# Second block: the gate-up product takes x without the norm's reciprocal root, which is multiplied onto each tile as it leaves PSUM

## The reference, cut to what matters

```python
def _rmsnorm(x, w):
    y = x * lax.rsqrt(jnp.mean(x * x, axis=-1, keepdims=True) + NORM_EPS)
    return y * w

def _conv_glu_ffn(h, ffn_up, ffn_conv, ffn_conv_bias, ffn_down):
    u = _causal_dwconv(h @ ffn_up, ffn_conv) + ffn_conv_bias    # 3 taps along the tokens
    gate, val = jnp.split(u, 2, axis=-1)                         # 2816 channels each
    return (jax.nn.gelu(gate, approximate=True) * val) @ ffn_down

# second_block, one layer
h = _hybrid_mixer_2(_rmsnorm(x, pre_mix_norm[l]), ...)
x = x + _rmsnorm(h, post_mix_norm[l])
h = _conv_glu_ffn(_rmsnorm(x, pre_ffn_norm[l]), ...)
x = x + _rmsnorm(h, post_ffn_norm[l])
```

## Time and profile before

| | |
|---|---|
| median of three runs | 1983.71 us |
| the profiled execution: time, span | 1979.94 us, 1978.1 us |
| busy share of the span: PE, DVE, ACT, POOL | 95%, 61%, 50%, 36% |
| mean granted TensorE clock | 0.975 |
| chain that ended last, by engine | PE 68%, DVE 10%, ACT 8%, DMA 6%, issue 5%, POOL 2% |
| bytes read from HBM | 309.61 MB |

### The profile page before, as it was taken

One profiled execution on the slowest core, in us unless ns is written; L12 is line 12 of the kernel. 1 busy time (PEld: TensorE's weight loads), 2 busy tenths in 40 slices (PEclk: granted clock), 3 DMA queues, 4 the chain that ended last, 5 costly groups with the idle time before them and its releaser, 6 DMA issues.

```text
span 1978.1 us, 40944 instructions
## 1 busy us (share of the span) xinstructions
PE 1880.3 (95%) x15728; PEld 1842.6 (93%) x15728; DVE 1214.3 (61%) x1480; ACT 993.4 (50%) x1301; POOL 722.0 (36%) x607
## 2 busy tenths in 40 slices
PE   6999999999999999999999998997999889979997
PEld 6999999999999999999999997987999889969997
DVE  5655586666556545676665566556774755647754
ACT  4434565454454345555544456455654464556542
POOL 4760211257317621303376102513661105215631
PEclk9999999999999999999999989998999889999999
DMA  6646444455465556344464633222555323215543
GB/s 228 201 167 212 171 150 150 154 194 205 157 206 192 184 165 210 129 153 168 171 210 156 200 136 107 86 86 86 199 185 165 135 104 107 87 50 180 196 153 125
DMA packets 48938, 312.33 MB, mean 158 GB/s; under 512 B 5680, under 2 KB 6832, under 8 KB 19888
## 3 DMA queue, kind: packets, MB, share of 16 engines
q1 hardware_dynamic: 48096, 307.84, 45.6%
q10 hardware_dynamic: 720, 2.84, 0.4%
HBM read 309.61 MB, written 1.05 MB: 157 GB/s over the span
## 4 chain that ended last, share of the span: by engine, by line
PE 68%; DVE 10%; ACT 8%; DMA 6%; issue 5%; POOL 2%; ACTq 0%; DVEq 0%; SPq 0%; POOLq 0%
PE ps L558 18%; PE ps L559 18%; PE ps L560 18%; DMA raw<-in_down_dram 4%; ACT w_hi_w L1215 4%; DVE w_lo_w L1695 4%; PE ps L915 3%; PE ps L563 3%; PE ps L565 3%; PE ps L564 3%; DMA raw<-in_in_dram 1%; DVE v L2244 1%; DVE conv L2023 1%; PE ps L726 1%; PE ps L766 1%
## 5 line engine op out<-in xcount | busy, mean ns | idle before, releaser
L1695 DVE TENSOR_TENSOR w_lo_w<-raw,w_hi_w 128x2048 fp32r<-128x2048 f32 (+1 forms) x288 | 616.3, 2140 | 303.0 <-ACT w_hi_w L1215 302.3
L558 PE MATMUL ps<-xn,w_hi_w 128*128 128x256 f32 x2688 | 762.6, 284 | 39.9 <-DVE xn L1709 26.4
L559 PE MATMUL ps<-xn,w_hi_w 128*128 128x256 f32 x2688 | 753.8, 280 | 0.0
L560 PE MATMUL ps<-xn,w_lo_w 128*128 128x256 f32 x2688 | 753.6, 280 | 0.0
L1215 ACT ACTIVATE w_hi_w<-raw 128x2048 fp32r<-128x2048 f32 (+1 forms) x288 | 497.8, 1730 | 141.0 <-DMA raw<-in_down_dram 89.9
L558 PEld LDWEIGHTS ps<-xn,w_hi_w 128*128 128x128 f32 x2688 | 515.9, 192 | 47.8 <-DVE xn L1709 24.1
L559 PEld LDWEIGHTS ps<-xn,w_hi_w 128*128 128x128 f32 x2688 | 514.6, 191 | 0.6 <-issue 0.5
L560 PEld LDWEIGHTS ps<-xn,w_lo_w 128*128 128x128 f32 x2688 | 514.2, 191 | 0.0
L558 PE MATMUL ps<-h,w_hi_w 128*128 128x256 f32 x1056 | 294.2, 279 | 3.0 <-DVE w_lo_w L1695 3.0
L560 PE MATMUL ps<-h,w_lo_w 128*128 128x256 f32 x1056 | 293.8, 278 | 0.0
L559 PE MATMUL ps<-h,w_hi_w 128*128 128x256 f32 x1056 | 293.8, 278 | 0.0
(11 more groups left out here) (336 smaller groups left out, 2822.1 us busy)
## 6 DMA issues: line engine op xcount, KB each, us to landing
raw<-in_gu_dram SPq DMA_DIRECT2D x132, 1024.0 KB, 4.9
raw<-in_in_dram SPq DMA_DIRECT2D x68, 1024.0 KB, 4.9
raw<-in_down_dram SPq DMA_DIRECT2D x96, 704.0 KB, 4.1
raw<-in_out_dram SPq DMA_DIRECT2D x16, 1024.0 KB, 4.8
raw<-in_pb_dram SPq DMA_DIRECT2D x4, 1024.0 KB, 4.9
raw<-in_pa_dram SPq DMA_DIRECT2D x4, 1024.0 KB, 4.9
tables_all<-in_tables_dram ACTq DMA_DIRECT2D x1, 1648.0 KB, 6.8
rows<-in_rows_dram SPq DMA_DIRECT2D x2, 768.0 KB, 5.5
```

What stands on the lines that cost most here:

```text
L558: pe.matmul(out, w, xh, start=first, stop=False)
L559: pe.matmul(out, w, xl, start=False, stop=False)
L560: return pe.matmul(out, wl, xh, start=False, stop=last)
L1695: dve.tensor_tensor(in_ring(w_lo_ring, at, k)[:, 0:elems], raw[:, k % RAW_RING, 0:elems], in_ring(w_hi_ring, at, k)[:, 0:elems], ALU.subtr ...
```

## The change

ACT now makes the high part of `x * gain` as soon as a chunk of x is there (`split_x`, together with the square), and DVE the low part (`scale_low`) inside `post(1)`; the two engines' second pass with `v` is gone, and POOL's part of it. POOL sums the eight squares (`post_square`), and PE multiplies that sum by one matmul between the two tiles of slot 1 instead of eight matmuls ahead of slot 0. The split of slot 2 (`open_rounds`) stands ahead of the root. In each round DVE first multiplies both tiles by `rstd` from PSUM into `conv_in`, and the second of these signals `drained`; the taps of ACT and DVE then read `conv_in`.

The core of the diff (the counts of semaphores and removed helpers are left out):

```diff
             mean_square(at, 0)
-            mean_square_direct(at, 1)
             first_wide(at, st2["gu"], 0)
+            def mean_of_x():
+                pe.wait_ge(post_sum.sem, post_sum.upto(at, KC - 1))
+                pe.matmul(ps[:, AUX, 0:T], ones_d[:], sq8[:, 0], start=True, stop=True).then_inc(mean_sq.sem, 1)
-            wide(at, st2["gu"], 1, 0, xn, KC)
+            wide(at, st2["gu"], 1, 0, xn, KC, None, mean_of_x)
...
             src = conv_in[:, j % 2, f]
+            if f == 0:
+                before = 6 if st.name == "gu" else 0
+                act.wait_ge(conv_src.sem, conv_src.upto(at, before + j + 1 + 4 * g))
+            else:
+                act.wait_ge(drained.sem, drained.upto(at, st.free0 + j + 1 + 4 * g))
             if st.name == "gu":
-                tile_done(act, at, st, j, f, g)
-                src = ps[:, 2 * (j % 2) + f, 0:T]
...
+                act.sem_inc(held.sem, 1)
...
             for c in range(KC):
                 x_ready(act, at, 0, c)
+                split_x(c, gains2[:, 4 * layer + 2, c:c + 1])
                 act.activation(sq8[:, c], x[:, c], ACT.Square).then_inc(squared.sem, 1)
+            open_rounds(at, st2["gu"], split)
             root(at, 2)
-            for c in range(KC):
-                act.wait_ge(v_ok.sem, v_ok.upto(at, c + 1))
-                copy(xn[:, c, 0], v[:, c]).then_inc(xn_hi.sem, 1)
...
-                whole = st.name == "gu"
-                if not whole:
-                    for f in range(2):
-                        tile_done(dve, at, st, j, f, g)
-                        dve.tensor_tensor(conv_in[:, j % 2, f], ps[:, 2 * (j % 2) + f, 0:T], rstd[:, 0:T], ALU.mult)\
-                           .then_inc((conv_src, drained)[f].sem, 1)
+                for f in range(2):
+                    tile_done(dve, at, st, j, f, g)
+                    dve.tensor_tensor(conv_in[:, j % 2, f], ps[:, 2 * (j % 2) + f, 0:T], rstd[:, 0:T], ALU.mult)\
+                       .then_inc((conv_src, drained)[f].sem, 1)
+                dve.wait_ge(drained.sem, drained.upto(at, st.free0 + j + 1 + 4 * g))
...
-                        src = ps[:, 2 * (j % 2) + f, 0:T - s] if whole else conv_in[:, j % 2, f, 0:T - s]
-                        ins = dve.scalar_tensor_tensor(c, src, w(f, last_tap - s), c, ALU.mult, ALU.add)
+                        dve.scalar_tensor_tensor(c, conv_in[:, j % 2, f, 0:T - s], w(f, last_tap - s), c,
+                                                 ALU.mult, ALU.add).then_inc(conv_ok.sem, 1)
...
                 def scale_next(c):
-                    if k == 3 and layer < DEPTH - 1:
+                    n = k // 2
+                    if k == 1 or layer < DEPTH - 1:
...
             split(at, so.slot0 + 3 + LEAD, 0, SLOT)
+            open_rounds(at, st2["gu"], split)
             inverse(at, 2)
-            for c in range(KC):
-                dve.scalar_tensor_tensor(v[:, c], x[:, c], gains2[:, 4 * layer + 2, c:c + 1], rstd[:, 0:T],
-                                         ALU.mult, ALU.mult).then_inc(v_ok.sem, 1)
-                if c >= 2 and c % 2 == 0:
-                    low_even(at, 0, c - 2)
-            low_even(at, 0, KC - 2)
...
-            add_odd(at, 0)
-            for c in range(1, KC, 2):
-                low(at, 0, c)
+            def post_square(c):
...
+                pool.tensor_tensor(sq8[:, 0], sq8[:, 0], sq8[:, c], ALU.add).then_inc(post_sum.sem, 1)
+            add_odd(at, 0, {3: (1,), 5: (2, 3), 7: (4, 5, 6, 7)}, post_square)
```

More of the change, by code:

```diff
@@ L362, in program @@
     col_ok = sig("col_ok", 0, 1)
-    v_ok = sig("v_ok", 0, KC)
+    post_sum = sig("post_sum", 0, KC - 1)
     post_v = sig("post_v", 0, 2 * KC)
@@ L421, in program @@
     tap = sig("tap", 0, 12 + 2 * FC)
-    conv_ok = sig("conv_ok", 0, 36 + 3 * FC)
-    conv_src = sig("conv_src", 0, 6)
+    conv_ok = sig("conv_ok", 0, 36 + 4 * FC)
+    conv_src = sig("conv_src", 0, 6 + FC)
     z_ok = sig("z_ok", 0, 1)
@@ L1668, in gelu @@
             def gelu(j, g):
-                act.wait_ge(conv_ok.sem, conv_ok.upto(at, 36 + 3 * j + 3 + 12 * g))
+                act.wait_ge(conv_ok.sem, conv_ok.upto(at, 36 + 4 * j + 3 + 16 * g))
                 act.activation(silu_gate[:, j % 2], conv[:, j % 2, 0], ACT.Gelu_apprx_tanh).then_inc(gate_ok.sem, 1)
             act.activation(warm[:, 3:4], eps[:, 0:1], ACT.Gelu_apprx_tanh)
-            open_rounds(at, st2["gu"], split)
             rounds(act, at, st2["gu"], SLOT_DOWN, FC, split, gate_taps, gelu)
@@ L2003, in taps @@
             def taps(st, j, g, w, slots0, conv0, last_tap):
-                whole = st.name == "gu"
-                if not whole:
-                    for f in range(2):
-                        tile_done(dve, at, st, j, f, g)
-                        dve.tensor_tensor(conv_in[:, j % 2, f], ps[:, 2 * (j % 2) + f, 0:T], rstd[:, 0:T], ALU.mult)\
-                           .then_inc((conv_src, drained)[f].sem, 1)
-                    dve.wait_ge(drained.sem, drained.upto(at, st.free0 + j + 1))
-                per = 2 * last_tap - (1 if whole else 0)
+                for f in range(2):
[3 more added lines that the diff above has]
+                dve.wait_ge(drained.sem, drained.upto(at, st.free0 + j + 1 + 4 * g))
+                if st.name == "gu":
+                    dve.sem_inc(held.sem, 1)
+                per = 2 * last_tap
                 for s in range(1, last_tap + 1):
@@ L2238, in scale_next @@
                 def scale_next(c):
-                    if k == 3 and layer < DEPTH - 1:
-                        x_ready(dve, at, 1, c)
-                        scale_low(at, 1, c, gains2[:, 4 * (layer + 1), c:c + 1], xn_lo_odd if c % 2 else xn_lo_even)
+                    n = k // 2
+                    if k == 1 or layer < DEPTH - 1:
+                        x_ready(dve, at, n, c)
+                        scale_low(at, n, c, gains2[:, 4 * layer + k + 1, c:c + 1], xn_lo_odd if c % 2 else xn_lo_even)
                 for c in range(KC):
@@ L2291, in add_square @@
             pool.tensor_tensor(ssum[:], ssum[:], sqb[:, c % 2], ALU.add).then_inc(summed.sem, 1)
-        def low(at, n, c):
-            pool.wait_ge(xn_hi.sem, xn_hi.upto(at, KC * n + c + 1))
-            pool.tensor_tensor(xn[:, c, 1], v[:, c], xn[:, c, 0], ALU.subtract).then_inc(xn_lo_odd.sem, 1)
         def add_squares(at, k):
@@ L2448, in _ @@
             add_squares(at, 0)
-            add_odd(at, 0)
-            for c in range(1, KC, 2):
-                low(at, 0, c)
+            def post_square(c):
+                pool.wait_ge(squared.sem, squared.upto(at, KC + c + 1))
+                if c > 1:
+                    pool.wait_ge(post_sum.sem, post_sum.upto(at, c - 1))
+                pool.tensor_tensor(sq8[:, 0], sq8[:, 0], sq8[:, c], ALU.add).then_inc(post_sum.sem, 1)
+            add_odd(at, 0, {3: (1,), 5: (2, 3), 7: (4, 5, 6, 7)}, post_square)
             split_h(at, st2["gu"], 0)
```

13 lines of the change are left out of this document (1 added, 12 removed).

## The result

The changed kernel takes 2000.96 us (median of 9 runs, 1992.7 to 2010.72), the kernel before 1983.71 us (9 runs, 1977.83 to 1990.25). The ratio is 1.0081, 95% interval [1.0056, 1.0105]: slower by about 16 us, outside the range forecast. The profiled execution has a span of 1999.6 us, 21.5 us more than before, at a granted clock of 0.976 (0.975 before).

The account below looks back on a forecast made before the run. PE's idle wait at each gate-up entry was taken as the bound. A layer: -3.5 at the entry, +1.3 in the rounds, +0.5 at the end, makes -1.7 us; two layers -3.4, so 1980.3 us from 1983.7; range 1974 to 1990.

Parts of the forecast that it names:

- the ring: Each gate-up round: DVE split, drain, ACT tap, ACT split, DVE split; 5.40 us, or 5.49 with the `held` count.
- A round, worked from 'qkv': Part reckoning a gate-up round from stage "qkv": 5.50 us against PE's 5.43, 18 times a layer, +1.3 us.
- The entry: Gate-up's start: first matmul 5.7 us after R, the mixer norm's reciprocal, instead of 14.2; slot 1 at R + 17.2.
- What slot 3 wins: Start of gate-up's slot 3: 3.5 us earlier a layer, or 4.4 us if POOL's two adds cost nothing.
- Drain to tap: Step of the ring from DVE's drain to ACT's tap: 0.45 us, plus 0.09 for the `held` count.
- Two taps to ACT's split: Step of the ring from the first of ACT's two taps to its split: 0.81 us, read from "qkv".
- DVE's own way and the collision: DVE's line through a gate-up round: 4.93 us, 5.49 with POOL's subtraction (0.46) and cast (0.1) beside its taps.
- The rival with two collisions: Gate-up rounds: POOL and DVE collide twice, 5.85 us a round, 9.2 us lost in all, 1993 us; chance 13%.
- The end: End of gate-up, before PE resumes in "down": one added drain loses 0.5 us a layer, bounds 0 and 1.
- The clock: Rival: PE falls to half clock in gate-up's slot 1, costing 1.7 us a layer; 1983.7 us, no change; chance 8%.
- The bounds: Gate-up round between 5.43 us (PE's own) and 6.08 us (all three POOL instructions land on DVE's way).
- The sign I had named: Stated test in the profile after: the forecast is wrong if a gate-up round is over 5.6 us.

Follow-up runs that it names:

- e4: Changed kernel with ACT's 22 gate-up rounds written out instead of looped: 1995.45 us, rounds 5.67 to 5.68 us.
- e9: Changed kernel with ACT's gate-up taps made without the convolution's bias: 1980.38 us, rounds 5.60 us in the loop and 5.49 behind it.
- e2: Changed kernel without the `held` counts in the taps on ACT and DVE: 2000.4 us, round 5.81 us.
- e10: Changed kernel with e2 and e4 together (no `held` counts, ACT's rounds written out): 1993.25 us, round 5.66 us.
- e1: Changed kernel with POOL's subtraction for the low part of h replaced by a cast: 1989.06 us, round 5.88 us.
- e3: Changed kernel with e1 and e2 together (POOL's cast, no `held` counts): 1998.17 us, round 5.81 us.
- e12: e11 with POOL's subtraction replaced by a cast, as in e1: 1990.17 us, round 5.47 us.
- e5: Changed kernel's entry with the rounds of the kernel before (taps read PSUM, root left out): 1982.43 us, ratio 0.9982 to the kernel before.
- e11: e10 with ACT's taps made without their bias, as in e9: 1988.09 us, round 5.47 us.
- e8: Changed kernel, ACT splitting one slot further ahead, DVE splitting between drains and taps, and slot 1 during the mixer's last tiles: 1981.27 us, ratio 0.9986.

## Why the prediction was wrong

The mechanisms were named rightly, and two terms of the ring that sets the round were too small. Both lie in "A round, worked from 'qkv'", and the third miss, at the end of the stage, follows from it in the main.

- **The entry, right within 0.6 us.** First matmul R + 5.7 forecast, 5.72 measured; slot 1 R + 17.2 and 17.23, idle 1.8 and 1.77. The root came 0.3 us later than reckoned (1376.76, R + 20.70), and the drain of slot 0 at R + 23.28 instead of R + 22.7. The 0.9 us for POOL's squares is there, but only half of it ahead of the split of slot 1: four xn instructions took 3.58 us instead of 3.09, so the split began at R + 14.35, not 14.8, and then took 2.82 us (the one behind it 2.28). That slot 1 came out exact is luck in this respect.
- **What slot 3 wins, 3.5 forecast, 2.2 measured.** 0.6 us is the later drain, and 0.4 the ring's two steps below, which stand in that sum too. The remaining 0.36 is a misreading of the kernel before: the sum has slot 2 start when ACT saw slot 1 done, at 1377.7, but PE went on at 1377.32 without a wait.
- **Drain to tap, 0.54 forecast, 0.73 measured.** It was read from "qkv", whose six rounds are written out. 16 of the 22 rounds here stand in a loop, and there drain to tap is 0.20 us longer (e4): 0.09 of it is the bias's (e9) and about 0.05 the `held` count's, which costs 0.07 in the loop (e2) and 0.02 outside it (e10). The forecast's 0.09 for the count, read in "down", was near the first. But without loop and count the step is 0.51, where "qkv" has 0.45.
- **Two taps to ACT's split, 0.81 forecast, 1.00 measured.** The tap in "qkv" has a scale, the tap here a scale and a bias. Two take 1.09 us instead of 0.91, and e9 gets the 0.19 back. The row of the right instruction stood in the earlier trace rows: 0.57 us for one, against 0.91 for two in the earlier trace rows. I didn't set them beside each other. The Trainium skill (page "ScalarE: Activation LUTs", section "What ACT_TABLE_LOAD costs") has the same: each operand that is a pointer to one value per partition adds about 93 ns to an activation. The two taps here agree, with 0.09 us more for each of them. 0.20 + 0.19 is the whole difference between 5.49 and 5.88; that it comes out so exactly is chance in part, as the count was taken too high outside the loop and the 0.45 too low.
- **DVE's own way and the collision.** Forecast 1.58 us for the four taps and 0.56 for POOL, 2.14 in all; from start to start they take 2.16. Two errors cancel: in round 0, where POOL is idle, their row is 1.78 us long instead of some 1.66, and POOL adds 0.45 to it (2.23). As forecast, one tap of the four is lengthened, to 1.05 us from 0.47. The step from ACT's first tap to DVE's was 0.77 instead of 0.61 as well. None of it decides, since ACT's way got longer (e1, e3, e12). The rule of the Trainium skill on it (page "SBUF — State Buffer", section "Who interferes with whom") agrees: taps with both operands in SBUF take 0.45 us more beside POOL's subtraction, while taps that read the tile from PSUM take 0.40 us each beside it (three in 1.27 us, e5) and as much where POOL is idle (four in 1.65). Beside POOL's cast, which reads SBUF too, the four take 1.84 us (e1), hardly more than alone. The rival with two collisions didn't occur: POOL's `hv` (1389.34) still starts 0.43 us behind DVE's split (1388.91).
- **The end, 0.5 forecast, 3.1 measured** (a wait of 4.28 instead of 1.21). I added one drain to a chain that began when PE's last tile ended. But DVE and ACT are now late themselves: the last tile ends at about 1497.1, its drain starts at 1498.57, and all four taps follow the drain. Some 1.0 us of it goes where POOL's subtraction is a cast (e1; e3 against e2), so that part is the collision's. What PE has lost in the rounds isn't lost beside the end, but on top of it. Where DVE and ACT have caught up with PE, the forecast's 0.5 is right: in layer 0 of e11 PE resumes 5.4 us after the end of its last tile, against 4.9 before and 8.0 in the changed kernel.
- **The clock** didn't fall in slot 1 of this profile (granted 1.00), though it fell behind the wait at the end, where the sum has no term for it. But the rival was real: of the 22 layers with this entry and its 1.8 us wait in all profiles, five have half clock in slot 1 (e1 and e3 in layer 0, e11 in layer 1, e9 in both), and there slot 2 starts at R + 25.7 instead of R + 24.1, 1.6 us later, where the rival reckoned 1.7. e1 (columns as in the windows above):

```profile
1366.70:1370.20 3.50, 3.50 (x20) 3.50 (x19) 1.64 (x1) 0.00 (x0) 0.00 (x0) 0.51 0.82 279
```

- **The bounds.** The upper end of 6.08 us for a round held, but all of it was POOL's, and the range was cut at a round of 5.7 us. The sign I had named ("wrong if a round is over 5.6 us") is what the profile shows, and the sum follows it: -2.2 at slot 3, +7.5 by the last tile (15 x 0.45 + 3 x 0.24), +3.1 at the end, 8.4 us a layer and 16.8 for both. The medians differ by 17.3. Part of that agreement is chance, since the half clock behind the end (1.6 us a layer) and PE's pace aren't in the sum.

The slip of method: the margin was 0.03 us (5.40 against 5.43, before the count), the ring has four steps, and 18 rounds twice multiply an error by 36. Each of its steps had to be read from an instruction of the same form, operands and loop.

## What to carry to other kernels

When a change spends an engine's head start, reckon the ring of dependences that is then exposed, step by step from start to start, and take each step from an instruction with the same operands (scale, bias, source) and the same kind of code (looped or written out). A gain at the entry of a stage is paid once; a loss in its round is paid every round and once more at the end. And when two engines must each wait for the other's split in one round, move one of the splits a slot ahead before anything is added to the round.

## What the runs showed of the hardware

TensorE has two paces at one granted clock. Windows in one SwiGLU stage of the first block, which is the same code in both kernels, first before, then after (same columns as above):

```profile
1100.00:1110.00 10.00, 10.00 (x91) 10.00 (x90) 5.60 (x5) 4.86 (x5) 0.74 (x1) 1.00 0.48 152
```

```profile
1100.00:1110.00 10.00, 10.00 (x87) 10.00 (x87) 5.37 (x7) 5.56 (x7) 0.74 (x1) 1.00 0.61 200
```

The granted clock is 1.00 in both, but 91 matmuls fall into 10 us in one and 87 in the other; their starts lie 0.113 and 0.118 us apart (1104.78 to 1106.48 in 15 steps; 1104.77 to 1106.42 in 14). One stage keeps one pace for most of its length, and which one it gets changes from stage to stage and run to run with no edit: this stage took 183.9 us between its norms' reciprocals before and 189.7 after. That is about the 5.5 us by which R was late in this comparison. In e5 the same stage took 189.7 us and R of layer 0 is 1370.61 instead of 1350.57, though its edit lies behind R. It is why the length of a round tells more than a whole time. The cause stays open. The Trainium skill (page "TensorE: Matmul & The Clock Gate", section "Wait — 56ns, not 53.3ns?") gives matmuls at the full clock their columns at 2.4 GHz and about 2.5 ns. An estimate from these figures is 109 ns for 256 columns; both paces measured here are slower than that. Where the ring sets the round, as after the change, the slower pace of 5.65 us a slot would be hidden below its 5.88. Where PE sets it, the pace shows in full: in e8 the last gate-up tile ends at R + 135.4 in layer 0, at the slower pace, and at R + 131.2 in layer 1.
